# Two low parts moved from the vector engine to ScalarE and an accumulating DMA, and an earlier turn of x, at three layer norms

## What is computed

```python
x = _layer_norm(x, ln_in_g, ln_in_b)
for l in range(DEPTH):                                   # DEPTH = 2
    mix = _mixer(x, w_in[l], b_f[l], w_pa[l], w_pb[l], w_pc[l], w_o[l])   # ends in merged @ w_o
    x = _layer_norm(DN_ALPHA * x + mix, ln1_g[l], ln1_b[l])
    ffn = _swiglu(x, w_gate[l], w_up[l], w_down[l])       # (silu(x @ gate) * (x @ up)) @ down
    x = _layer_norm(DN_ALPHA * x + ffn, ln2_g[l], ln2_b[l])
return x
```

## Time and profile before

| | before |
|---|---|
| median of 3 runs | 873.73 us (873.67 to 873.92) |
| the profiled execution | 873.21 us, span 871.4 us |
| granted TensorE clock | 0.998 |
| TensorE matmul busy | 839.7 us (96%), 4216 instructions |
| VectorE busy | 513.4 us (59%), of which low parts of weights (L857) 309.0 us |
| ScalarE busy | 400.3 us (46%), of which w_hi casts (L759) 257.4 us |
| GpSimd busy | 56.9 us (7%) |
| HBM read | 147.60 MB, 171 GB/s over the span |

### The profile page before, as it was taken

How to read it: one execution, slowest core, us unless ns; L and a number is a source line. 1 busy time by engine, 2 the same in 40 slices (tenths; PEclk the granted TensorE clock), 3 DMA queues, 4 the chain that set the end, 5 groups by cost and what they waited for, 6 DMA issues and landing times.

```text
span 871.4 us, 10732 instructions
## 1 busy us (share of the span) xinstructions
PE 839.7 (96%) x4216; PEld 695.1 (80%) x4216; DVE 513.4 (59%) x728; ACT 400.3 (46%) x536; POOL 56.9 (7%) x86
## 2 busy tenths in 40 slices
PE   2999999999999999999999999999999899999995
PEld 2888888888877888888878889888888688888884
DVE  6565464556796545445685656463778764555436
ACT  3476465543344344444336655554443453343430
POOL 0012331000000000000000324200000000000000
PEclk9999999999999999999999999999999999999999
DMA  9574433456646765654436443435754576556501
GB/s 319 172 255 159 133 125 114 137 181 229 193 145 206 229 193 184 202 194 150 153 110 229 142 160 103 141 106 181 240 178 145 191 247 202 189 182 193 193 0 49
DMA packets 93458, 149.35 MB, mean 171 GB/s; under 512 B 3424, under 2 KB 52832, under 8 KB 93408
## 3 DMA queue, kind: packets, MB, share of 16 engines
q1 hardware_dynamic: 93408, 148.66, 52.5%
HBM read 147.60 MB, written 1.05 MB: 171 GB/s over the span
## 4 chain that ended last, share of the span: by engine, by line
PE 89%; DVE 7%; DMA 2%; ACT 1%; issue 1%; SPq 0%; ACTq 0%; DVEq 0%
PE bank L1041 79%; PE bank L1100 3%; DVE w_lo L857 3%; PE bank L1056 3%; PE bank L1132 2%; DMA raw<-in_w_in 2%; PE bank L1120 1%; PE bank L1066 1%; ACT w_hi L759 1%; DVE x L1007 1%; DVE x L1004 1%; DVE stats L974 1%; DVE x L971 1%; DVE act_lo L862 1%; DVE newton L991 0%
## 5 line engine op out<-in xcount | busy, mean ns | idle before, releaser
L857 DVE TENSOR_TENSOR w_lo<-raw,w_hi 128x2048 fp32r<-128x2048 f32 (+3 forms) x142 | 309.0, 2180 | 91.6 <-ACT w_hi L759 91.1
L1041 PE MATMUL bank<-w_hi,act_hi 128*128 128x512 f32 (+2 forms) x864 | 342.4, 396 | 3.6 <-DVE act_lo L862 3.4
L1041 PE MATMUL bank<-w_hi,act_lo 128*128 128x512 f32 (+2 forms) x864 | 332.9, 385 | 0.0
L1041 PE MATMUL bank<-w_lo,act_hi 128*128 128x512 f32 (+2 forms) x864 | 331.6, 384 | 0.0
L759 ACT CAST w_hi<-raw 128x2048 fp32r<-128x2048 f32 (+3 forms) x142 | 257.4, 1814 | 125.8 <-PE bank L1041 100.3
L1041 PEld LDWEIGHTS bank<-w_hi,act_hi 128*128 128x128 f32 x864 | 162.9, 189 | 33.6 <-DVE act_lo L862 3.8
L1041 PEld LDWEIGHTS bank<-w_hi,act_lo 128*128 128x128 f32 x864 | 162.6, 188 | 32.9
L1041 PEld LDWEIGHTS bank<-w_lo,act_hi 128*128 128x128 f32 x864 | 163.1, 189 | 28.8
L1041 PE MATMUL bank<-w_hi,y_hi 128*128 128x512 f32 x240 | 95.2, 397 | 0.0
L1041 PE MATMUL bank<-w_hi,y_lo 128*128 128x512 f32 x240 | 93.6, 390 | 0.0
L1041 PE MATMUL bank<-w_lo,y_hi 128*128 128x512 f32 x240 | 93.5, 389 | 0.0
(11 more groups left out here) (88 smaller groups left out, 551.5 us busy)
## 6 DMA issues: line engine op xcount, KB each, us to landing
raw<-in_w_in SPq DMA_DIRECT2D x48, 1024.0 KB, 5.2
raw<-in_w_gate SPq DMA_DIRECT2D x44, 512.0 KB, 3.9
raw<-in_w_up SPq DMA_DIRECT2D x44, 512.0 KB, 5.0
raw<-in_w_down SPq DMA_DIRECT2D x22, 1024.0 KB, 4.9
raw<-in_w_o SPq DMA_DIRECT2D x8, 1024.0 KB, 5.2
raw<-in_w_in SPq DMA_DIRECT2D x4, 768.0 KB, 4.3
raw<-in_w_pa SPq DMA_DIRECT2D x4, 768.0 KB, 4.4
raw<-in_w_pc SPq DMA_DIRECT2D x4, 768.0 KB, 4.4
```

Of the source, the lines that this page charges most:

```text
L857: dve.tensor_tensor(weights(w_lo, i, HI_SLOTS), weights(raw, i, RAW_SLOTS), weights(w_hi, i, HI_SLOTS).bitcast(F32), ALU.subtract).then_in ...
L1041: ins = pe.matmul(bank[use[0]][:, 0:width], a, w[:, k, c0:c0 + width], start=start and k == 0 and p == 0, stop=stop and k == nk - 1 and p ...
```

## The change

The diff has two parts. First, for the pieces that `low_part_by_dma` names (gu(1,0) and gu(1,1) in both layers, qkv(1,0) and qkv(1,1) in layer 1: six of 142), the vector engine's subtraction is gone. ScalarE, right after its cast of raw to w_hi, writes the negative of raw, rounded to fp32r, into w_lo; GpSimd then issues a DMA that adds raw to it in place, so that w_lo is again raw less its rounded value. The DMA's completion is counted by `lo_by_dma`; GpSimd issues one only after the one before has landed. TensorE, and SP's loads into the raw buffer, wait for that count where they waited for `lo_done`. Second, turn_x(0, 1) is placed directly behind turn_x(0, 0), ahead of the last 12 matmuls of tile 1, at the three inner norms.

```diff
+def low_part_by_dma(layer, name):
+
+    return name in (("gu", 1, 0), ("gu", 1, 1)) or layer > 0 and name in (("qkv", 1, 0), ("qkv", 1, 1))
...
                     if t == 1 and half == 1 and n == 1:
-                        turn_x(0, 0)
+                        turn_x(0, 0, 1)
                     mm(at[("wo", half, n)], t, ("act", 4 * half), [(wo_use[t][n], 0, NW, half == 0, half == 1)],
...
             if t:
-                turn_x(0, 1)
                 split_to(at[("gu", 1, 1)])
...
                 if c == last and t == TT - 1 and layer < DEPTH - 1:
-                    turn_x(0, 0)
+                    turn_x(0, 0, 1)
                 down(c, t, t == TT - 1)
             if t and layer < DEPTH - 1:
-                turn_x(0, 1)
                 split_to(base[layer + 1] + 3)
...
+        def wait_lo(engine, i):
+
+            if i in dma_count:
+                engine.wait_ge(lo_by_dma, 16 * dma_count[i])
+            else:
+                engine.wait_ge(lo_done, dve_count[i])
...
                     if i >= RAW_SLOTS:
-                        sp.wait_ge(lo_done, i - RAW_SLOTS + 1)
+                        wait_lo(sp, i - RAW_SLOTS)
...
+                if step[0] == "lo" and step[1] in dma_count:
+                    i = step[1]
+                    if dma_count[i] > 1:
+                        pool.wait_ge(lo_by_dma, 16 * (dma_count[i] - 1))
+                    pool.wait_ge(minus_hi_done, dma_count[i])
+                    pool.dma_start(weights(w_lo, i, HI_SLOTS), weights(raw, i, RAW_SLOTS),
+                                   accum_op=ALU.add).then_inc(lo_by_dma, 16)
...
                     act.copy(weights(w_hi, i, HI_SLOTS), weights(raw, i, RAW_SLOTS)).then_inc(hi_done, 1)
+                    if i in dma_count:
+                        act.mul(weights(w_lo, i, HI_SLOTS), weights(raw, i, RAW_SLOTS), -1.0
+                                ).then_inc(minus_hi_done, 1)
...
-                if kind == "lo":
+                if kind == "lo" and step[1] in dve_count:
                     i = step[1]
                     dve.wait_ge(hi_done, i + 1)
...
                     pe.wait_ge(drained[lb], ln)
-                    pe.wait_ge(lo_done, i + 1)
+                    wait_lo(pe, i)
```

More of the change, by code:

```diff
@@ L586, in trunk @@
         lo_done = sem("lo_done")
+        lo_by_dma = sem("lo_by_dma")
+        minus_hi_done = sem("minus_hi_done")
         piece_used = sem("piece_used")
@@ L610, in trunk @@
         out_done = sem("out_done")
+        dma_count, dve_count = {}, {}
+        for layer, order in enumerate(orders):
+            for n, name in enumerate(order):
+                mine = dma_count if low_part_by_dma(layer, name) else dve_count
+                mine[base[layer] + n] = len(mine) + 1
+        def wait_lo(engine, i):
[3 more added lines that the diff above has]
+                engine.wait_ge(lo_done, dve_count[i])
         raw_count, so_far = [], [0] * RAW_SLOTS
@@ L708, in _ @@
             for step in PLAN:
-                if step[0] == "spread" and step[6] is not None and step[6]["rope"]:
+                if step[0] == "lo" and step[1] in dma_count:
[5 more added lines that the diff above has]
+                                   accum_op=ALU.add).then_inc(lo_by_dma, 16)
+                elif step[0] == "spread" and step[6] is not None and step[6]["rope"]:
                     ev = step[6]
```

## The result

The changed kernel takes 897.38 us (median of four runs, 895.96 to 898.18) against 873.70 us on the same chip (873.00 to 873.92): a ratio of 1.0271, with a 95% interval of 1.0253 to 1.0288. It is 2.7% slower. The forecast was 882 us with 867 to 893 around it: the sign was right, the time lies above the range.

What follows compares the result with a forecast made beforehand. TensorE, busy in 96% of the span, was taken as the bound, with waits for the vector engine at three inner norms; slowdowns of 2.6 + 2.6 + 2.8 = 8.0 us on 873.7 gave 882 us, range 867 to 893.

Steps and rivals of the forecast that it cites:

- The ceiling: At the three inner norms: without TensorE's waits for the vector engine, at most 7.3 us come back, giving 866.4 us.
- A: The norm after layer 0's output projection; could give 3.2 us, forecast 2.6 us slower with the adding DMAs.
- B: The norm after layer 0's FFN; could give 0.9 us at most, forecast 2.8 us slower with the adding DMAs.
- C: The norm after layer 1's output projection; same as A: could give 3.2 us, forecast 2.6 us slower.
- The early turn: Tile 0's second half turned before the last 12 matmuls: free at A and C; at B those matmuls start 1.26 us later.
- The vector engine and ScalarE: At A, statistics start about 250.2, not 254.19, first half ready 2.2 us before TensorE asks; ScalarE's negative takes 1.92 us.
- The DMA at B: Second add lands 15.4 us after the negative, at 453.7, 3.7 us after TensorE needs it; little is loaded beside.
- The DMA beside loads: At A and C: two adds take 15.4 us plus 1.25 for sharing; at A TensorE waits 5.8 us.
- As fast as a copy: Rival for the adds at all three norms: D up to 5.2 us, whole 7.3 us come back, 866.4 us; chance 0.28.
- The estimate of 6.8 us: D for one add from the skill's pages: 2.0 + 4.8 us, the point from which the change is slower, contention left out.
- Sharing hits in full: Rival: adding transfer slow or sharing in full at the norms, D = 10, 19.4 us slower, 893 us; chance 0.20.
- D: Time of one accumulating 1 MB DMA issued by GpSimd at the inner norms, taken as 7.7 us.

Runs made afterwards that it cites:

- the filled kernel: The changed kernel with useless matmuls (34 at A and C, 16 at B) where TensorE waits for the second add: 892.40 us, ratio 1.0214 to the kernel before.
- the first two kernels with GpSimd's subtractions: Changed kernel without negative and DMA; GpSimd subtracts all six low parts, in one instruction per piece (877.23 us) or four of 512 columns (873.24 us).
- overlapped adds: The changed kernel with GpSimd issuing the second add once its negative is there, not after the first has landed: 878.91 us, ratio 1.0050 to the kernel before.
- the first GpSimd kernel: The changed kernel without negative and DMA; GpSimd makes each of the six low parts with one subtraction: 877.23 us, ratio 1.0043 to the kernel before.
- the best split: Against the changed kernel: GpSimd subtracts gu(1,0) and qkv(1,1), the vector engine gu(1,1) among tile 1's statistics; early turn only at A and C: 866.24 us.

## Why the prediction missed

**The ceiling: right.** 3.2 + 3.2 + 0.9 us give 866.4; the add left out gives 865.7, with A, B and C shorter by 3.3, 1.0 and 3.3 us.

**The early turn: right.** Free at A and C, and at B a new idle (0.69 us measured before the second half's turn).

**The vector engine and ScalarE: right.** Statistics at A start 2.97 us after the turns (251.27 - 248.30) where 3.3 was forecast (250.2 - 246.91); tile 1's first turn has no wait; the negative takes 1.91 us.

**The DMA at B: right.** Two adds were put at 15.4 us and take 15.0 (449.19 to 464.18), and TensorE waits 3.47 us where 3.7 was forecast.

**The DMA beside loads: the step that failed.** "Each such load is 2.4 us of all engines. I charge half of one, 1.25 us, at A and C; at B little is loaded." The two adds at A took 9.8 + 11.1 = 20.9 us, not 15.4 + 1.25 = 16.65: 4.3 us more; those at C took 20.1, 3.4 more. With the loads made small they take 14.8. The load pays too. The second load of gu(2,0), issued just behind the second add, landed after 9.9 us, where the median of its kind is 5.0 (the load of down(0), issued 0.7 us ahead of the first add, took 5.4 in place of 4.9). I had the argument in hand (the earlier trace rows shows the loads that would fall together with the adds, and the prediction speaks of the next load starting with the second) and still charged half of one load for both.

**The clock: a term that was missing.** I summed the waits as time that only passes. After each of them TensorE ran 9 to 12 matmuls 0.43 us apart: 6.5 us by the rows, 5.0 by the filled kernel. Sharing alone would have made the sum 890, inside the range; the clock takes it past 893. The clock is also the whole of B's miss: 2.8 forecast, 5.2 measured, 2.4 of it in that block.

Together: 8.0 forecast + 8.4 for the sharing (4.5 at A, 3.9 at C: what is left of their 9.0 and 8.7 after the forecast's 2.6 and the clock's 1.9 and 2.2) + 6.5 for the clock + 1.4 before A = 24.3, the difference of the spans.

**The rivals.** "As fast as a copy" had 0.28 and fell on both counts: the add isn't, and a copy wouldn't have won here (1.0058). The estimate of 6.8 us from the Trainium skill's pages "DMA: Bandwidth & Descriptors" and "Collectives: The Full Stack" is near what an add alone took (7.3 to 7.5), and its rule of two source reads agrees with the trace, where an add alone took 2.5 us more than a copy; the estimate says nothing of an add beside loads, and by it the time would have come out even. "Sharing hits in full", D = 10, at a chance of 0.20, was the mechanism that came true at A and C (10.5 and 10.0 us for each add of a pair), but not at B (7.5); its 893 left the clock out as well.

## What to carry to other kernels

Price a transfer on a critical path by what else the DMA engines carry in that stretch, the loads that its own landing sets free included, and count both it and them as slowed; here two adds grew from 14.8 us to 20.9. A wait of several microseconds in a stream of matmuls can cost more than its length: of the twelve waits of 2.6 to 7.9 us at A, B and C in these kernels, TensorE came back at half its clock behind ten. When an engine's chain has several links that could leave it, test them together: the turn alone was worth nothing, and 4.8 us once the low parts had gone. And look at every place that a variant touches: the first two kernels with GpSimd's subtractions lost their time at B, not where the first held instruction was found.

## What the runs showed of the hardware

- The clock behind a wait isn't a matter of that wait's length alone. At B of the kernel with small loads the matmuls behind 3.40 us of idle ran 0.23 us apart (clock 1.00 in 456.05 to 461); at A, behind 3.96 us, 0.43 apart; with overlapped adds at A, 3.24 us were enough for 0.43, with another 1.88 us of idle that had ended 3.4 us before; at B of the kernel with four subtractions per piece, 2.58 us were enough (clock 0.60 in 439.80 to 444). What decides between them is open.
- Two adds in flight, beside loads, finished 4.8 us sooner at A than one behind the other, though the median add took longer (9.8 us, not 9.2); without loads they gained nothing (15.0 us both ways).
- GpSimd subtracts 128 x 2048 in 4.62 us where it starts ahead of the vector engine's instruction (B of the first GpSimd kernel), and in 5.6 to 5.8 us where it starts while a subtraction of the vector engine still runs (246.31 to 252.12 at A of the best split, beside one until 247.61); the vector engine needs 2.28. All instructions of the vector engine that were held beside it were scalar_tensor_tensor with two SBUF tensors; with one input from the bank the same operation was not.
- GpSimd is busy 0.86 to 1.01 us with the issue of each add, and 0.53 to 0.72 with that of a copy.
